# Hybrid attention and convolution block on eight cores: evictions ahead of a batched attention epilogue, one signal per set of copies, openings with a unit ahead, and a merge in attention's tile order

## The reference, cut to what matters

```python
proj = h @ w_in                                          # (B,S,D_IN), S = 2048, D_MODEL = 1024
q, k, v, g_attn, glu, g_conv, gates = split(proj)
# branch A: 4 heads, two softmaxes each, T5 bias, causal
p = softmax(q1 k1' * scale + bias) - lam * softmax(q2 k2' * scale + bias)
o = rms_norm(p @ v, subln_w) * (1 - lambda_init)         # per head
y_attn = (o * silu(g_attn)) @ w_attn_proj
# branch B: GLU, causal depthwise convolution of width 31, layer norm over channels
u = a * sigmoid(bgate)
u = layer_norm(causal_depthwise_conv(u, conv_w, conv_b))
y_conv = (silu(u) * silu(g_conv)) @ w_conv_proj + b_conv_proj
# merge
merged = sigmoid(gate_attn) * y_attn + sigmoid(gate_conv) * y_conv
h = layer_norm(alpha * h + merged @ w_out)
```

## Time and profile before

| | us |
|---|---|
| median of 3 runs | 828.47 (828.14 to 833.8) |
| the profiled execution, its own time | 826.72 |
| its span on core 4 | 825.1 |
| spans of all cores | 812.6 to 825.1 |
| PE busy / DVE / ACT / POOL | 645.5 / 334.4 / 306.9 / 122.9 |

### The profile page before, as it was taken

How to read it: one execution, slowest core, us unless ns; L and a number is a source line. 1 busy time by engine, 2 the same in 40 slices (tenths; PEclk the granted TensorE clock), 3 DMA queues, 4 the chain that set the end, 5 groups by cost and what they waited for, 6 DMA issues and landing times.

```text
span 825.1 us, 12929 instructions; the slowest of 8 cores (812.6 to 825.1 us)
## 1 busy us (share of the span) xinstructions
PE 645.5 (78%) x4192; PEld 314.0 (38%) x4192; DVE 334.4 (41%) x780; ACT 306.9 (37%) x446; POOL 122.9 (15%) x139
## 2 busy tenths in 40 slices
PE   2799998966669677386964856656899999999982
PEld 0244444533324344143532423332344444444431
DVE  1122411153341624515245244556123573663746
ACT  0011114645633466344544534452122341432413
POOL 4000100010210102101021000121422122222211
PEclk9899999988969897898887988887899999999997
DMA  7971371110021100311001100406790231211322
GB/s 98 163 131 47 60 120 30 50 32 1 15 51 36 48 1 2 66 28 47 10 0 28 28 2 1 77 0 110 154 195 4 72 133 52 94 59 52 103 76 102
DMA packets 28749, 49.07 MB, mean 59 GB/s; under 512 B 6123, under 2 KB 20364, under 8 KB 28300
## 3 DMA queue, kind: packets, MB, share of 16 engines
q0 software_dynamic: 8672, 19.93, 15.5%
q1 hardware_dynamic: 20012, 28.32, 11.3%
HBM read 50.13 MB, written 9.18 MB: 72 GB/s over the span
## 4 chain that ended last, share of the span: by engine, by line
PE 62%; DVE 11%; issue 7%; DMA 7%; SPq 7%; ACT 2%; POOL 1%; DVEq 1%; ACTq 0%; POOLq 0%
PE pd L526 18%; PE pd L1215 7%; PE pd L1137 7%; PE pd L1139 7%; SPq L681 7%; PE pd L950 4%; PE pd L696 4%; PE pd L1143 3%; PE pd L1141 3%; PE pd L920 3%; DMA wh<-w_head 3%; PE pd L550 3%; DMA u<-upad 2%; DVE od L979 2%; DMA wcp<-w_conv_proj 2%
## 5 line engine op out<-in xcount | busy, mean ns | idle before, releaser
L937 ACT ACTIVATE pT<-pd 128x1024 bf16<-128x1024 f32 (+3 forms) x160 | 140.2, 896 | 105.4 <-PE pd L928 65.9
L526 PE MATMUL pd<-xT,wh 128*128 128x512 bf16 x384 | 106.7, 430 | 58.6 <-DVE ycf L704 47.9
L950 PE MATMUL pd<-vaug,pT 128*128 128x130 bf16 x1088 | 94.1, 229 | 13.0 <-ACT osb L519 12.9
L950 PEld LDWEIGHTS pd<-vaug,pT 128*128 128x128 bf16 x1088 | 73.8, 103 | 47.7 <-issue 37.6
L526 PEld LDWEIGHTS pd<-xT,wh 128*128 128x128 bf16 x384 | 38.4, 107 | 110.6 <-issue 83.4
L1137 PE MATMUL pd<-xT,wg 128*128 128x512 bf16 x256 | 61.8, 385 | 12.0 <-DMA wcp<-w_conv_proj 10.0
L1147 ACT ACTIVATE sg<-pd 128x512 f32<-128x512 f32 x32 | 19.1, 597 | 129.9 <-PE pd L1143 111.2
L1150 DVE TENSOR_TENSOR sg<-pd,sg 128x512 f32<-128x512 f32 x32 | 22.1, 690 | 97.2 <-ACT sg L1147 77.8
L920 PE MATMUL pd<-qT,kT 64*128 64x512 bf16 (+3 forms) x320 | 59.2, 366 | 2.6 <-ACT qT L519 1.4
L1215 PE MATMUL pd<-wout,mergedT 128*128 128x512 bf16 x256 | 57.9, 386 | 3.9 <-POOL mergedT L1155 3.9
L1139 PE MATMUL pd<-xT,wg 128*128 128x512 bf16 x256 | 60.5, 379 | 0.0
(11 more groups left out here) (113 smaller groups left out, 784.3 us busy)
## 6 DMA issues: line engine op xcount, KB each, us to landing
xres<-x SPq DMA_DIRECT2D x16, 512.0 KB, 4.7
y<-hres SPq DMA_DIRECT2D x16, 512.0 KB, 2.8
u<-upad SPq DMA_DIRECT2D x192, 33.8 KB, 1.8
wg<-w_gate POOLq DMA_DIRECT2D x8, 512.0 KB, 11.7
wh<-w_head POOLq DMA_DIRECT2D x4, 768.0 KB, 13.6
xT<-xt POOLq DMA_DIRECT2D x3, 1024.0 KB, 34.6
u<-upad SPq DMA_DIRECT2D x64, 33.7 KB, 1.9
wab<-w_ab POOLq DMA_DIRECT2D x4, 512.0 KB, 22.1
```

Of the source, the lines that this page charges most:

```text
L526: ins = e.matmul(ps[bank][:, :], w[:, c, c0:c0 + 128], xT[:, c, t * 512:(t + 1) * 512], start=(c == 0), stop=(c == KC - 1))
L937: S.add("act", lambda e: e.activation(out=pT2[pi][:, :, 0:ncol], in_=pdv[:, :, 0:ncol], func=AF.Exp, scale=SCALE), writes=[("pT", pi)], ba ...
L950: ins = e.matmul(ps[bank][:, col:col + 130], pT2[pi][:, c, rr * 128 - c0:(rr + 1) * 128 - c0], vaug[:, j, h, :], start=(j == 0 and first), ...
```

## The change

1. In the loop `run_late(i)` now stands ahead of `emit_pv` and `drain`.
2. The epilogue's chunks are batched over the four row groups: DVE and POOL operations of 128x4x128 elements with broadcast factors in place of 12 + 4 operations of 128x128; two products of 512 columns (L982, L988 of the new kernel) go to POOL. At most one chunk is written per step, two when two tiles are pending. The transpose is written two steps after the last chunk.
3. `load_u4` ends with a `nop` on SP that waits for the 16 copies; the convolution waits for that one signal. The last 30 columns of a tile of `upad` have a key of their own (`ut`), so that `silu` no longer waits for the next tile's copies.
4. The value products of a tile's first key block are three operations, one per bank. No unit is written in the step ahead of a tile's first value product (`nxt_first`), so that one can stand right before it.
5. The last product of `gc_unit` goes from DVE to POOL.
6. `wap` lies where `u4` and `qT` were and is loaded with `wcp` after the last statistics unit; `wg[5]`, `wg[6]` lie where `wab` was. The loads of `wh` come at the tail of `ga_units` instead of in the next head.
7. What is left of the units and the epilogue's chunks are written in turns (`tick`). The merge takes the tiles in `torder`, and the late loads are written two per merge unit.

```diff
@@ a_unit, load_u4, conv_unit, silu
-              reads=[("th", i)], writes=[("u", m, t)], banks=[B(bank)])
+              reads=[("th", i)], writes=[("u", m, t), ("ut", m, t)], banks=[B(bank)])
...
-                    reads=["upad0"] + [("u", cc, tt) for tt in range(max(0, t - 1), t + 1)],
-                    writes=[("u4", sl, gl, sh)], dma=True)
+                    reads=["upad0", ("u", cc, t)] + ([("ut", cc, t - 1)] if t > 0 else []),
+                    writes=[("u4", sl, gl, sh)], dma=True, after=[("u4all", sl)])
+        S.add("sp", lambda e: e.nop(), reads=[("u4", sl, gl, sh) for gl in range(4) for sh in range(4)], writes=[("u4all", sl)])
...
-        S.add("pe", cv, reads=["w4", ("u4z", sl)] + [("u4", sl, gl, sh) for gl in range(4) for sh in range(4)], banks=[B(FB)])
+        S.add("pe", cv, reads=["w4", ("u4z", sl), ("u4all", sl)], banks=[B(FB)])
...
-                  after=[("u", cc, tt) for tt in range(max(0, t - 1), t + 1)])
+                  after=[("u", cc, t)] + ([("ut", cc, t - 1)] if t > 0 else []))
@@ gc_unit
-            S.add("dve", lambda e: e.tensor_tensor(out=u, in0=u, in1=th[i][:, :], op=ALU.mult),
+            S.add("pool", lambda e: e.tensor_tensor(out=u, in0=u, in1=th[i][:, :], op=ALU.mult),
@@ groups
-        spread(conv_units(3), spread(tail_of(ga_units(3), chain(*[do(load_wg, m, wh_all) for m in range(3)])), gc_units(0) + gc_units(1))),
+        spread(tail_of(conv_units(3), chain(load_wcp, load_wap)), spread(ga_units(3), gc_units(0))) +
+        tail_of(gc_units(1), chain(*[do(load_wg, m, wh_all) for m in range(3)])),
@@ emit_pv
-        S.add("pe", pv, reads=[("pT", pi), ("v", j), ("vones", j)], banks=[B(b) for b in ACCB])
+        for banks in ([[b] for b in ACCB] if j == 0 else [ACCB]):
+            S.add("pe", lambda e, banks=banks: pv(e, banks), reads=[("pT", pi), ("v", j), ("vones", j)], banks=[B(b) for b in banks])
@@ tile_epilogue
+        def c_o1():
+            S.add("dve", lambda e: e.tensor_tensor(out=od[ob][:, :, :], in0=osb_[:, 0:4, 0:128], in1=bc(rs[ob][:, 0:4]), op=ALU.mult),
+                  reads=[("rs", ob)] + okeys, writes=[("od", ob)])
+            S.add("pool", lambda e: e.tensor_tensor(out=osb_[:, 4:8, 0:128], in0=osb_[:, 4:8, 0:128], in1=bc(rs[ob][:, 4:8]), op=ALU.mult),
+                  reads=[("rs", ob)] + okeys, writes=[("o2", ob)])
+        def c_o2():
+            S.add("dve", lambda e: e.tensor_tensor(out=od[ob][:, :, :], in0=od[ob][:, :, :], in1=osb_[:, 4:8, 0:128], op=ALU.add),
+                  reads=[("o2", ob)], writes=[("od", ob)])
+            S.add("pool", lambda e: e.tensor_tensor(out=osb_[:, 0:4, 0:128], in0=od[ob][:, :, :], in1=od[ob][:, :, :], op=ALU.mult),
+                  reads=[("od", ob)], writes=[("o1", ob)])
...
+        chunks.extend([c_o1, None, c_o2, None, c_ssq, None, c_f1, c_f2])
@@ the loop over the steps
+        nxt_first = i + 1 >= LOOK and i + 1 - LOOK < len(steps) and steps[i + 1 - LOOK][2] == 0
+        due = not nxt_first and i < len(steps) and groups[h] and (n_units - len(groups[h]) + 0.5) * total < done * n_units
...
+        run_late(i)
         if i >= LOOK:
             emit_pv(i - LOOK)
-            drain(4)
-        run_late(i)
+        drain(1 if len(pending) < 2 else 2)
@@ after the loop
+    rest[-1] = chain(rest[-1], do(load_wg, 3, ["wgc"]), do(load_wg, 4, ["wgc"]))
+    left = [(f, 2) for f in groups[3]] + [(f, 1) for f in rest]
+    while left:
+        f, n = left.pop(0)
+        f()
+        tick(n)
...
+    for ti in range(NTT):
         for m in range(KC):
-            merge_unit(m, t)
+            merge_unit(m, ti)
+            for _ in range(2):
+                if loads:
+                    loads.pop(0)()
```

More of the change, by code:

```diff
@@ L384, in build @@
     BT8 = A.alloc("BT8", [128, 4, 2, 128], BF16)
+    epi_off = A.p
     NOB = 2
@@ L388, in build @@
     od = [A.alloc("od", [128, 4, 128], F32) for _ in range(NOB)]
-    osq = [A.alloc("osq", [128, 128], F32) for _ in range(4)]
-    osqc = [0]
     ssq = [A.alloc("ssq", [128, 4], F32) for _ in range(NOB)]
@@ L824, in load_wap @@
         S.add("pool", lambda e: e.dma_start(out=wap[:, :, :], in_=wap_d), writes=["wap"], dma=True,
-              after=[("ycf", 1, cc) for cc in range(4)])
+              after=[("u4all", sl) for sl in range(NU4)] + [("u4z", sl) for sl in range(NU4)])
     def load_wcp():
@@ L943, in emit_pv, with pv @@
         r, c0, pi = info.pop(i)
-        def pv(e):
+        def pv(e, banks=ACCB):
             ins = None
@@ L949, in pv @@
                     bank, col, first = acc_loc(c, rr)
+                    if bank not in banks:
+                        continue
                     ins = e.matmul(ps[bank][:, col:col + 130], pT2[pi][:, c, rr * 128 - c0:(rr + 1) * 128 - c0],
@@ L964, in tile_epilogue @@
             S.add("act", copy_on("act", osb_[:, 3 * bi:3 * bi + na, :], ps[bank][:, 0:na * 130].rearrange("p (a e) -> p a e", a=na)),
-                  writes=[("o", ob, bi)], banks=[B(bank)])
+                  writes=[("o", ob, bi)], banks=[B(bank)], after=[("o1", ob), ("o2", ob)])
         okeys = [("o", ob, bi) for bi in range(3)]
-        chunks = []
+        chunks = [None]
         def c_rs():
@@ L1010, in tro @@
                 return ins
-            S.add("pe", tro, reads=[("oab", tb, rr) for rr in range(4)] + ["ident"], banks=[B(FB)])
+            S.add("pe", tro, reads=[("oab", tb), "ident"], banks=[B(FB)])
             s = sgac[(h, t)]
@@ L1085, in build @@
         return nc
-    wg.extend([A.alloc("wg", [128, KC, 256], BF16) for _ in range(5, KC)])
+    wg.extend([A.alloc("wg", [128, KC, 256], BF16) for _ in range(7, KC)])
     wout = A.alloc("wout", [128, KC, D], BF16)
@@ L1096, in build @@
     xres = [A.alloc("xres", [128, D], F32) for _ in range(NXR)]
-    hres = [A.alloc("hres", [128, D], F32) for _ in range(NSL)]
     junk = [A.alloc("junk", [128, D], BF16) for _ in range(2)]
@@ L1166, in resid @@
                                                           op0=ALU.mult, op1=ALU.add, accum_out=bst[sl][:, 0:1]),
-                  reads=[("xres", xs)], writes=hk + [("bst0", sl)], banks=[B(b0), B(b0 + 1)])
-            if n + NXR < NTB:
-                load_xres(n + NXR)
+                  reads=[("xres", xs)], writes=hk + [("bst0", sl)], banks=[B(b0), B(b0 + 1)],
+                  after=epi_keys if k < NSL else [])
+            if k + NXR < NTB:
+                load_xres(k + NXR)
         def square():
-            S.add("act", lambda e: e.activation(out=junk[n % 2][:, :], in_=hres[sl][:, :], func=AF.Square, scale=D ** -0.5,
+            S.add("act", lambda e: e.activation(out=junk[k % 2][:, :], in_=hres[sl][:, :], func=AF.Square, scale=D ** -0.5,
                                                 accum_out=bst[sl][:, 2:3]),
-                  reads=hk, writes=[("junk", n % 2), ("bst2", sl)])
+                  reads=hk, writes=[("junk", k % 2), ("bst2", sl)])
         def rstd_():
@@ L1217, in mo @@
                     return ins
-                S.add("pe", mo, reads=[("mg", c, t % 2) for c in range(KC)] + [("wout", c) for c in range(KC)], banks=[B(b0 + hf)])
-            inflight.append(block_stages(n, b0))
+                S.add("pe", mo, reads=[("mg", c, ti % 2) for c in range(KC)] + [("wout", c) for c in range(KC)], banks=[B(b0 + hf)])
+            inflight.append(block_stages(k, b0))
             advance()
-    for t in range(NTT):
+    for ti in range(NTT):
         for m in range(KC):
-            merge_unit(m, t)
-            if t > 0 and m in (1, 3):
-                out_unit(t - 1, m // 2)
+            merge_unit(m, ti)
+            for _ in range(2):
+                if loads:
+                    loads.pop(0)()
+            if late or pending or deferred_tr:
+                tick(2)
+            if ti > 0 and m in (1, 3):
+                out_unit(ti - 1, m // 2)
     out_unit(NTT - 1, 0)
```

112 lines of the change are left out of this document (47 added, 65 removed).

## The result

The changed kernel takes 712.7 us (four runs, 712.5 to 712.9) where the kernel before, run beside it, takes 828 to 834; the ratio is 0.8585, with a 95% interval of 0.8545 to 0.8626. All times and ratios are of fast runs: in some others, whatever the kernel, the cores of one die take some per cent longer at a lower granted clock. The forecast was 710 us. The spans of its cores are 704.8 to 711.1 us, at a mean granted clock of 0.96 to 0.97 (0.90 to 0.91 before). The rows here are of core 1, the slowest.

The account below looks back on a forecast made before the run. PE's waits in attention were taken as the bound: 126.5 (first stage) + 274 (attention's products) + 38 (remainders) + 12 (lower clock) + 5 (end of attention) + 251.3 (merge) = 706.8 us; forecast 710, own range 680 to 745 us.

Parts of the forecast that it names:

- What bounds it: Attention, 452.9 us between first stage and merge: bound by what PE waits for, not engine work; 179 us open to change.
- Evictions ahead of the epilogue: Attention, DVE's queue: putting evictions before the tile's epilogue removes the cause of nearly all 82 us of PE waits on FB.
- What stays on bank FB: Attention, 16 tiles: 0.5 us each for FB's next user and 0.5 us each for the batched epilogue, 8 + 8 us.
- the term for ACT: Attention, after each `var_unit`: table loads, logarithm, exponential and tanh among the exponentials cost PE 3 us a head, 12 us.
- One signal: Attention's convolutions: PE's 23.7 us of waits for 16 copies fall to one wait per convolution, 2.4 us in all.
- SP's loss of 2 us in the last head: Attention's last head: SP, held until a set of copies lands, delays two convolutions in a row, 2 us lost.
- Openings: Attention, tile starts: of 12.9 us that PE waits for ACT's copies of three banks, 3 stay.
- Sum of the remainders: Attention: waits of PE that stay after the change, 8 + 8 + 2.4 + 2 + 3 + 3 + 12 = 38 us (bounds 15 and 90).
- Lower clock: Attention: of 41 us of PE's busy time put down to the lower granted clock, 12 stay.
- the rival at 0.2: Attention: DVE's waits for POOL's epilogue products reach FB's evictions, 50 us more, 760 us; chance 0.2.
- End of attention: Attention to merge: waits of 5.7 and 10.0 us go; POOL's gate and other products leave 5 us (3 to 12).
- Merge: Last stage: release waits for `wg[3]`, `wg[4]`; third unit waits 4 us longer, restart costs 1.6 us: 245.7 to 251.3 us.

## Why the prediction was right, and where it wasn't

- **What bounds it**: right. The span lost 114.0 us; attention gave 120.8, and the merge took 6.8 back.
- **Evictions ahead of the epilogue** was named as what takes away "nearly all 82 us". That step failed as a cause. By itself it gives 7 us, and PE still waited 37.3 us for L704; what did it is the pace, which the prediction mentions only as something that hides POOL's waits. Pace alone gives 57 us, batching 10 more, and the place 10 in the end, when the others are there. The reading of the earlier trace rows was right (the eviction was late behind 15 operations), but the conclusion skipped a step: an operation that is written first in its step still queues behind what the steps before put there. The number held because all three were in the change; as a forecast for the place it would have been far off.
- **What stays on bank FB**: predicted 8 + 8 us evenly over 16 tiles. Measured some 22 us, but in other places: 10.0 of them in four waits for the gate's eviction after a variance, which was where the term for ACT (12 us) was put. There it wasn't ACT's tables alone: with silu's wait gone from DVE's queue, 5.8 us of the 10.0 went.
- **One signal**: right, 2.4 us predicted to stay, 0.3 us measured. The 23.7 us of waits in the earlier trace rows were worth 27 us alone and 23.5 undone. SP's loss of 2 us in the last head isn't seen.
- **Openings**: the wait for ACT's copies was put at 3 us and is gone, but scores wait 9.3 us for exponentials in its place. Of 10 us predicted, 6 are measured, and they show as clock and not as idle time.
- **Sum of the remainders**: 38 us and 5 for the end of attention predicted, 41.5 us idle. The sum agrees better than its terms: 22 us on bank FB for 28 (with ACT's 12) and 12 us at the scores for 6 nearly cancel, which is luck. **Lower clock**: 12 of 41 left predicted; 290.6 - 274 = 17 measured.
- **POOL** (the rival at 0.2): DVE was idle for POOL for 17.3 us in all, where the rival needed 50. Its waits in attention:

```profile
DVE od L1001 <- POOL rstd L997: 6.9, 11, 1.3
...
DVE ssq L992 <- POOL osb L988: 6.1, 5, 1.3
...
DVE od L986 <- POOL osb L982: 4.3, 4, 1.1
```

 The Trainium skill (SBUF — State Buffer, Who interferes with whom) has the later instruction block fully. The traces agree: in all 11 meetings of DVE's multiply with its twin the later one was put off to 0.12 to 0.15 us ahead of the other's end. The prediction read this right; on this multiply it cost little, 0.18 us a tile on average (0.93 for 0.75).
- **End of attention**: 5 us predicted, 3.0 + 3.3 measured (POOL's gate product, and a last transpose waiting for the epilogue).
- **Merge**: 251.3 us predicted, 252.5 measured; 5 to 7 us predicted at the third unit, 6.1 measured. The size was right, the mechanism in part. ACT began 5.5 us after PE's first unit (470.80 against 465.26), and 2.9 us after it where the loads were out of the release: so the two late loads are worth some 2.6 us (an estimate; 4 predicted). ACT's table load adds 1.3 us; the trace of the kernel before has none there. The other 2 us, which the kernel before had too, are the reading of signals. With the signals collected as well the whole wait is gone.

## What to carry to other kernels

When an eviction is late in an in-order queue, count what the steps before it have queued, not only what stands beside it in its own step. Spread the long sequence over steps first, then order within a step. Where several waits come together at one instruction, let an idle engine gather them into one signal, at stage boundaries as well as in the loop. Ask of each wait on a busy engine whether an earlier one already implies it: silu's cost 13 us. And when two engines share work, look at single pairs in the timeline; a mean can look like overlap where there is none.

## What was not expected of the hardware

Reading signals that are long there costs time, some 0.05 to 0.1 us each on every engine. All of these are estimates, from the rows above and the counts of signals in the kernels' programs:

- PE: the 16 of a convolution cost some 1.7 us (15.6 + 8.1 us in 14 waits), 0.1 us each.
- DVE: the 16 of a silu cost 1.2 us, 0.07 us each. At the release 46 signals fewer brought its start from 3.9 to 0.7 us behind ACT's sigmoid, again 0.07 us each.
- ACT: at the release 48 signals fewer brought its start from 2.9 to 0.3 us behind PE's first unit, 0.055 us each.
- SP: it went from 1.3 to 0.1 us behind POOL's last product with 24 signals fewer, 0.05 us each.

The kernel writes PE's signal first among ACT's waits and ACT's first among DVE's, so the reading starts only when these have come, and the costs of the engines add up: 2.6 + 3.2 us, of which PE saw 5.1 at its third unit. Whether the differences between the engines are real was not tried.
